# First loads, first norm and the mixer's projections as one program without barriers

## The reference, cut to what matters

```python
def rmsnorm(x, w):
    xf = x.astype(jnp.float32)
    y = xf * lax.rsqrt(jnp.mean(xf * xf, axis=-1, keepdims=True) + NORM_EPS)
    return (y * w.astype(jnp.float32)).astype(x.dtype)

def hybrid_mixer(h, w_in, ...):
    proj = (h @ w_in).astype(f32)
    ...

x = x + hybrid_mixer(rmsnorm(x, norm_mix_w[l]), w_in[l], ...)
x = x + memory_cross_attention(rmsnorm(x, norm_xa_w[l]), rmsnorm(mem, norm_mem_w[l]), ...)
x = x + peer_ffn(rmsnorm(x, norm_ffn_w[l]), ...)
```

## Time and profile before

| | us |
|---|---|
| median of 3 runs | 2443.94 |
| lowest and highest | 2443.73 to 2445.16 |
| profiled execution, its own time | 2442.29 |
| its span, first to last instruction | 2440.5 |
| PE busy | 2268.1 (93%) |
| DVE busy | 1551.4 (64%) |
| ACT busy | 1128.0 (46%) |

### The profile page before, as it was taken

One profiled execution on the slowest core, in us unless ns is written; L12 is line 12 of the kernel. 1 busy time (PEld: TensorE's weight loads), 2 busy tenths in 40 slices (PEclk: granted clock), 3 DMA queues, 4 the chain that ended last, 5 costly groups with the idle time before them and its releaser, 6 DMA issues. The chain is left out here.

```text
span 2440.5 us, 38520 instructions
## 1 busy us (share of the span) xinstructions
PE 2268.1 (93%) x15466; PEld 2085.1 (85%) x15466; DVE 1551.4 (64%) x2831; ACT 1128.0 (46%) x1966; POOL 74.5 (3%) x36
## 2 busy tenths in 40 slices
PE   5968888989999999999998999999999999878998
PEld 5967766989999998888887998979998899856998
DVE  5866354699888896666665546665546445494554
ACT  4532334444555445555554444444443444384443
POOL 0021000401000000000000000000000000000000
PEclk9988989989999999999998999999999999888999
DMA  5453232445444445656645555535555655303552
GB/s 219 148 67 79 104 138 73 158 143 174 155 147 148 147 148 164 196 192 194 194 156 217 189 189 208 193 135 209 188 192 183 232 184 185 118 18 121 190 187 106
DMA packets 78151, 389.74 MB, mean 160 GB/s; under 512 B 9739, under 2 KB 12683, under 8 KB 49580
## 3 DMA queue, kind: packets, MB, share of 16 engines
q1 hardware_dynamic: 76668, 383.13, 45.2%
q0 software_dynamic: 1040, 4.19, 1.6%
q10 hardware_dynamic: 288, 0.26, 0.0%
HBM read 382.31 MB, written 5.24 MB: 159 GB/s over the span
## 5 line engine op out<-in xcount | busy, mean ns | idle before, releaser
L246 DVE TENSOR_TENSOR split_slots<-ring,split_slots 128x1024 fp32r<-128x1024 f32 x396 | 468.2, 1228 | 333.1 <-ACT split_slots L237 333.1
L339 PE MATMUL banks<-x_transposed_hi,split_slots 128*128 128x256 f32 x1936 | 553.7, 286 | 14.9 <-PEq L417 5.7
L340 PE MATMUL banks<-x_transposed_lo,split_slots 128*128 128x256 f32 x1936 | 551.9, 285 | 0.0
L341 PE MATMUL banks<-x_transposed_hi,split_slots 128*128 128x256 f32 x1936 | 551.6, 285 | 0.0
L237 ACT ACTIVATE split_slots<-ring 128x1024 fp32r<-128x1024 f32 x406 | 404.3, 1049 | 222.1 <-PE banks L341 194.0
L350 DVE SCALAR_TENSOR_TENSOR expert_lo<-ring,expert_hi 128x512 fp32r<-128x512 f32 x512 | 360.3, 709 | 190.2 <-ACT expert_hi L345 189.1
L345 ACT ACTIVATE expert_hi<-ring 128x512 fp32r<-128x512 f32 x512 | 323.1, 632 | 276.5 <-PE banks L341 276.4
L339 PEld LDWEIGHTS banks<-x_transposed_hi,split_slots 128*128 128x128 f32 x1936 | 374.9, 194 | 17.8 <-issue 10.2
L340 PEld LDWEIGHTS banks<-x_transposed_lo,split_slots 128*128 128x128 f32 x1936 | 374.9, 194 | 1.5
L341 PEld LDWEIGHTS banks<-x_transposed_hi,split_slots 128*128 128x128 f32 x1936 | 374.8, 194 | 0.0
L339 PE MATMUL banks<-x_transposed_hi,expert_hi 128*128 128x256 f32 x1024 | 296.8, 290 | 17.7 <-DVE expert_lo L350 17.2
(11 more groups left out here) (468 smaller groups left out, 3469.2 us busy)
## 6 DMA issues: line engine op xcount, KB each, us to landing
ring<-in_ffn_w SPq DMA_DIRECT2D x132, 1024.0 KB, 4.8
ring<-in_peer_u SPq DMA_DIRECT2D x128, 512.0 KB, 3.5
ring<-in_peer_v SPq DMA_DIRECT2D x128, 512.0 KB, 4.2
ring<-in_w_in SPq DMA_DIRECT2D x16, 1024.0 KB, 5.0
ring<-in_sgu_w_in SPq DMA_DIRECT2D x16, 1024.0 KB, 4.8
ring<-in_peer_wq SPq DMA_DIRECT2D x8, 1024.0 KB, 5.1
ring<-in_sgu_w_out SPq DMA_DIRECT2D x8, 1024.0 KB, 4.7
ring<-in_kv_w SPq DMA_DIRECT2D x6, 1024.0 KB, 4.9
```

The lines of the kernel that those rows point to most:

```text
L246: ins = dve.tensor_tensor(self.parts[:, b, 1, p], self.k.w.slot(g)[:, p], self.parts[:, b, 0, p].bitcast(F32), ALU.subtract)
L339: pe.matmul(out, lh, rh, start=start, stop=False)
L340: pe.matmul(out, lh, rl, start=False, stop=False)
L341: return pe.matmul(out, ll, rh, start=False, stop=stop)
```

## The change

The three first stages share one block (`joined_stages`), so their two barriers are gone. x comes in two transfers, one for each tile, each with a semaphore of its own. The norm's weight is loaded as a row, spread over all partitions, into a part of `s.conv` that is not used yet, and is multiplied in while the row is scaled, on DVE before the transposes (`scalar_tensor_tensor`, two halves for each tile), where it was four instructions on the turned banks. The split of xT then reads PSUM directly. ident is asked for by ACT. The parameter columns and ones are asked for behind the ring slots and waited for where they are first used, and the mask constants and tables behind ring slots 3 to 5. Two of the four banks are split high before slot 0 and two behind it. Panel 0 runs by `high_first`. The lines behind the touched functions shift: in the changed kernel the transposes are line 513, and the matmuls of panel 0 are lines 320, 322 and those of `high_first`'s second loop.

```diff
--- before.py
+++ after.py
@@ -463,33 +463,41 @@
-def begin_program(k, s, bias, padded):
...
+class Begun:
+    def __init__(self, k):
+        self.x_landed = [k.sig.new() for _ in range(TILES)]
+        self.ident_landed, self.gain_landed, self.cols_landed, self.ones_landed, self.zeroed = (k.sig.new() for _ in range(5))
+        self.high, self.written = (k.sig.new() for _ in range(2))
+def begin_program(k, begun, gain, bias, padded):
+    a, block = k.a, k.open
+    consts = a["constants"].rearrange("p (c n) -> p c n", n=P)
+    @block.sync
+    def _(sp):
+        for i in range(TILES):
+            sp.dma_start(k.x[:, i, :], a["x"][0][i * P:(i + 1) * P, :]).then_inc(begun.x_landed[i], 16)
+        sp.dma_start(gain, a["norm_mix_w"].partition_broadcast(P).rearrange("p a d -> p (a d)")).then_inc(begun.gain_landed, 16)
+        k.w.issue(sp, RING)
+        sp.dma_start(k.cols[:, :], a["parameter_columns"]).then_inc(begun.cols_landed, 16)
+        sp.dma_start(k.ones[:, :], consts[:, C_ONES, :]).then_inc(begun.ones_landed, 16)
+    @block.scalar
+    def _(act):
+        act.dma_start(k.ident[:, :], consts[:, C_IDENT, :]).then_inc(begun.ident_landed, 16)
+    @block.vector
+    def _(dve):
+        dve.memset(k.eps[:, 0:1], EPS).then_inc(k.boot, 1)
+        dve.memset(k.eps[:, 1:2], LN_EPS).then_inc(k.boot, 1)
+        dve.memset(padded[:, :, 0:3], 0.0).then_inc(begun.zeroed, 1)
+        dve.memset(bias.table[32:33, :], NEG).then_inc(begun.zeroed, 1)
 COL_MIX, COL_XA, COL_MEM, COL_FFN, COL_CONV, COL_B1 = 0, 8, 16, 24, 32, 112
@@ -508,74 +516,52 @@
             ins.then_inc(ready, 1)
-def norm_transpose(k, jobs, loads=()):
...
+def first_norm(k, ctx, begun, xn, gain):
+    block = k.open
+    stat = k.sb(ctx, "row_stats", [P, 3, TILES])
+    warm = k.sb(ctx, "unused_root", [P, 1])
+    squared, rooted, recip, normed, banks = (k.sig.new() for _ in range(5))
+    highs, lows = split_turned(k, 4, k.xT, banks, begun.high, begun.written)
+    begin = Beginning(k)
+    @block.scalar
+    def _(act):
+        act.wait_ge(k.boot, 2)
+        act.activation(warm[:, :], k.eps[:, 0:1], ACT.Sqrt)
+        for i in range(TILES):
+            act.wait_ge(begun.x_landed[i], 16)
+            act.activation(xn[:, i, :], k.x[:, i, :], ACT.Square, accum_out=stat[:, 0, i:i + 1]).then_inc(squared, 1)
+            act.wait_ge(squared, i + 1)
+            act.activation(stat[:, 1, i:i + 1], stat[:, 0, i:i + 1], ACT.Sqrt, bias=k.eps[:, 0:1], scale=1.0 / D
+                           ).then_inc(rooted, 1)
+        highs(act, 0, 2)
+        begin.highs(act)
+        highs(act, 2, 4)
+    @block.vector
+    def _(dve):
+        for i in range(TILES):
+            dve.wait_ge(rooted, i + 1)
+            dve.reciprocal(stat[:, 2, i:i + 1], stat[:, 1, i:i + 1]).then_inc(recip, 1)
+            if i == 0:
+                dve.wait_ge(begun.gain_landed, 16)
+            dve.wait_ge(recip, i + 1)
+            for n in range(2):
+                own = slice(n * D // 2, (n + 1) * D // 2)
+                dve.scalar_tensor_tensor(xn[:, i, own], k.x[:, i, own], stat[:, 2, i:i + 1], gain[:, own],
+                                         ALU.mult, ALU.mult).then_inc(normed, 1)
+        lows(dve, 0, 2)
+        begin.lows(dve)
+        lows(dve, 2, 4)
+    @block.tensor
+    def _(pe):
+        pe.wait_ge(begun.ident_landed, 16)
+        for i in range(TILES):
+            turn_chunks(pe, k, xn[:, i, :], i, banks, 4, normed)
 def bank4(k, b):
@@ -589,13 +575,13 @@
 def split_turned(k, first, dst, banks, high, written):
-    def highs(act):
-        for b in range(4):
+    def highs(act, at=0, end=4):
+        for b in range(at, end):
             act.wait_ge(banks, b + 1)
             split_high(act, dst.hi[bank_part(b)], bank4(k, first + b)).then_inc(high, 1)
-    def lows(dve):
-        for b in range(4):
+    def lows(dve, at=0, end=4):
+        for b in range(at, end):
             dve.wait_ge(high, b + 1)
             split_low(dve, dst.lo[bank_part(b)], bank4(k, first + b), dst.hi[bank_part(b)]).then_inc(written, 1)
     return highs, lows
@@ -845,7 +831,7 @@
 MIXER_PANELS = 16
-def project_and_normalise(k, s, padded, memT):
+def project_and_normalise(k, s, begun, bias, padded, memT):
@@ -885,6 +871,10 @@
             for n, name in enumerate(("gdn_dt_bias", "gdn_a_log", "mlstm_i_bias", "mlstm_f_bias")):
                 sp.dma_start(row[:, n, :], k.a[name].partition_broadcast(P).rearrange("p a h -> p (a h)")
                              ).then_inc(gates_landed, 16)
+            k.w.issue(sp, 2 * RING)
+            sp.dma_start(s.consts[:, :, :], k.a["constants"].rearrange("p (c n) -> p c n", n=P)).then_inc(k.masks_landed, 16)
+            sp.dma_start(bias.table[0:32, :], k.a["rel_table_2"]).then_inc(k.table_landed, 16)
+            sp.dma_start(bias.onehot[:, :], k.a["bucket_onehot"]).then_inc(k.table_landed, 16)
             k.stream(sp)
         @block.tensor
@@ -894,6 +884,13 @@
                     pe.wait_ge(panel_read, m - 3)
                 split.ready(pe, m)
                 wh, wl = split.panel(m)
+                if m == 0:
+                    own = [slice(j * P, (j + 1) * P) for j in range(2)]
+                    high_first(pe, Before(None, (begun.high, 4), (begun.written, 4)),
+                               lambda j: k.psum[:, 0, j * SEQ:(j + 1) * SEQ],
+                               lambda j, c: ((wh[:, c, own[j]], wl[:, c, own[j]]), k.xT.at(slice(0, P), c)), True
+                               ).then_inc(split.eaten, 1)
+                    return
                 for j in range(2):
                     own = slice(j * P, (j + 1) * P)
                     for c in range(DC):
@@ -915,6 +912,7 @@
             def norms():
                 pe.wait_ge(squared, 2)
+                pe.wait_ge(begun.ones_landed, 16)
                 for b in KEYS_FIRST:
                     if b == 0:
                         pe.wait_ge(narrow_read, 1)
@@ -1028,7 +1026,6 @@
         @block.gpsimd
         def _(pool):
-            k.sig.clear_other(pool)
             pool.wait_ge(mem_low, 4)
             for n in range(2):
                 pool.wait_ge(shaped, 2 * n + 2)
@@ -1041,6 +1038,9 @@
         def _(dve):
             def convolve(item):
                 dve.wait_ge(panel_read, item + 1)
+                if item == 0:
+                    dve.wait_ge(begun.zeroed, 1)
+                    dve.wait_ge(begun.cols_landed, 16)
                 for tap in range(4):
                     for q in range(2):
                         n = 2 * item + q
@@ -3616,10 +3616,14 @@
             memT = Split(k, core, "memory_T", [P, DC, SEQ])
             with ExitStack() as inner:
                 padded = k.sb(inner, "conv_input_T", [P, 20, 3 + SEQ])
-                begin_program(k, s, bias, padded)
                 inner.enter_context(k.lasting_splits())
-                norm_transpose(k, [(k.x, k.xT, COL_MIX)])
-                project_and_normalise(k, s, padded, memT)
+                rows = s.conv[:, 0:12, :].rearrange("p a n -> p (a n)")
+                gain, xn = rows[:, 0:D], rows[:, D:3 * D].rearrange("p (i d) -> p i d", i=TILES)
+                with k.joined_stages():
+                    begun = Begun(k)
+                    begin_program(k, begun, gain, bias, padded)
+                    first_norm(k, inner, begun, xn, gain)
+                    project_and_normalise(k, s, begun, bias, padded, memT)
             s.more(k, core)
             key_query_products(k, s, bias)
             gdn_prepare(k, s, bias)
@@ -3647,7 +3651,7 @@
 _NAMES = ["x", "mem", "gdn_a_log", "gdn_dt_bias", "gdn_norm_w", "mlstm_i_bias", "mlstm_f_bias",
-          "mlstm_norm_w", "norm_xa_w", "norm_ffn_w", "peer_v", "norm_final_w", "rel_table_2", "ln_g_2", "ln_b_2", "sgu_ln_g_2",
+          "mlstm_norm_w", "norm_mix_w", "norm_xa_w", "norm_ffn_w", "peer_v", "norm_final_w", "rel_table_2", "ln_g_2", "ln_b_2", "sgu_ln_g_2",
           "sgu_ln_b_2", "sgu_b_s_2", "cmp_w2_2"]
```

More of the change, by code:

```diff
@@ L508, in turn_chunks @@
             ins.then_inc(ready, 1)
-def norm_transpose(k, jobs, loads=()):
[L514 to L569, removed]
-        @block.tensor
-        def _(pe):
-            for e in range(TILES * N):
-                n, i = divmod(e, TILES)
-                pe.wait_ge(normed, e + 1)
-                turn_chunks(pe, k, xn[n][:, i, :], i, banks, 4 * n)
-        k.idle_pool(block)
```

## The result

| us | before | changed |
|---|---|---|
| median | 2443.84 | 2427.97 |
| lowest to highest (4 runs each) | 2443.44 to 2445.16 | 2425.51 to 2430.28 |
| profiled execution, its own time | 2442.29 | 2430.28 |
| its span | 2440.5 | 2428.5 |
| first matmul of panel 0, in the profile | 28.13 | 14.64 |

The ratio is 0.9937, with a 95% interval of 0.9925 to 0.9949: faster, by 15.9 us in the median. The 2429.7 forecast lies inside its spread. Two later series of the same kernel gave medians of 2430.54 and 2429.68 (5 runs each) against 2444.36 and 2444.64 for the kernel before. Over all 14 runs the median of the changed kernel is 2429.6.

The account below looks back on a forecast made before the run. PE bounds the panels, but ahead of them 9 us are a wait for bytes and 13 us an ACT and DVE chain. Panel 0 starts at 13.9, not 28.13: 2443.94 - 14.2 = 2429.7, range 2426.5 to 2433.5.

Parts of the forecast that it names:

- The place: Stage ahead of panel 0: its first matmul comes 14.2 us earlier, and everything behind follows PE and shifts as a whole.
- The arrival: First loads: tile 0 seen landed at 4.25, tile 1 at 5.75, weight row at 7.0, slot 0 at 10.1.
- The sum for the row: Weight row's landing, behind x: 1.25 us after the transfer ahead of it, taken as 7.0.
- What I costed at nothing: Table load, tile 1's sums, late low parts, mem, later slots and constants: all covered by other work, 0 us.
- the sum: Chain from loads to panel 0: first matmul at 13.9 instead of 28.13, median 2429.7; chance 0.55 for 2428 to 2431.5.
- the order of passes: Panel 0 by high_first: low parts of banks 2 and 3 are free; in the old order it starts 1.4 us later.
- The clock: Panel 0 starts at 1.2 GHz for as long as before, no difference; bounds 1.9 us gained, 1.5 us lost.
- Rival B: Panel 0 starts at full clock after only 2.55 us idle: 1.9 us more gained, 2427.8; chance 0.22.
- the rule weighed in the prediction: Ahead of panel 0: transposes do not count as PE busy, so panel 0 starts low, 2429.7; against it, 2427.8.
- A: First landings share the engines, the row landing with slot 0 at 10.1: 11.2 us gained, 2432.7; chance 0.19.
- D: Whole program: more time at 1.2 GHz behind short idle times; 40 us more gives 2449.7; chance 0.02.
- The number: Whole kernel: profiled execution 2428.1, median 2429.7.

Follow-up runs that it names:

- The barrier run: Changed kernel with the barrier between the first norm and the panels put back, SP waiting there for ones and the columns: 2432.01 us.
- the third series: Second repeat of the changed kernel with no edit, on the same chip as later experiments: median 2429.68 us.

## Why the prediction was right

**The place.** Right: all of the gain is ahead of panel 0, the work behind it is PE's and moves along, and ones behind the weights was the largest part (7.7 of 13.4 us by a run of its own).

**The arrival** was the term that was mis-sized. Tile 0's square began at 4.83 (forecast 4.25), the row was there at 7.78 (7.0), slot 0 at 2.14 + 8.1 = 10.24 (10.1). The rate of the earlier trace rows held from 4 to 6 us, but the microsecond after it has a hole:

```profile
4.00:6.00 2.00, 0.00 (x0) 0.00 (x0) 0.00 (x0) 1.15 (x2) 0.00 (x0) 1.00 1.03 407
6.00:7.00 1.00, 0.00 (x0) 0.00 (x0) 0.16 (x1) 0.99 (x2) 0.00 (x0) 1.00 0.74 238
```

The same microsecond in the kernel before:

```profile
6.00:7.00 1.00, 0.00 (x0) 0.00 (x0) 0.00 (x0) 0.00 (x0) 0.00 (x0) 1.00 0.87 369
```

What makes the hole is not shown. The sum for the row also left out ident's 0.07 MB, which landed at 0.75 + 4.2 = 4.95, ahead of it. And the two later loads that it was taken from were asked for 0.38 us apart (299.29 and 299.67) and not 0.45, which makes the second 1.2 us behind the first and not 1.25. The 0.78 us of the row went through the chain nearly unchanged: transposes at 8.68 for 7.85, slot 0's low half until 14.59 for 13.9, first matmul 14.64 for 13.9. So 13.5 us and not 14.2. The durations taken from rows held: scaling 1.41 for 1.42, transposes 3.65 for 3.49, splits 1.99 and 2.36.

**What I costed at nothing** was nothing: table load, tile 1's sums, low parts of banks 2 and 3, mem, slots 1 to 5, constants. The barrier run adds that mem could come 11 us later still and slot 3 four.

**Two steps reasoned past each other.** I gave x by tiles a landing of its own in the sum, though the sum itself shows tile 0 waiting for the row. The run with x in one transfer gives it 0.2 us. And I counted the order of passes as 1.4 us and the barriers as part of the whole; the runs show panel 0 starting 1.3 us later with the old order alone and 1.4 with the second barrier alone, so either of the two takes the whole saving away.

**The clock.** The sum took panel 0 as starting low for 4.2 us, with 1.9 us gained or 1.5 lost as bounds. Its length in the profiles was 8.37, 8.45 and 7.32 us against 7.70 before: 0.7 us lost, 0.8 lost and 0.4 gained, within the bounds. Rival B as written (all of panel 0 at full clock) came true in no profile without extra matmuls on PE; of the three of the changed kernel one started fast and fell. That the transposes leave the clock low, the rule weighed in the prediction (the Trainium skill, "TensorE: Matmul & The Clock Gate", "Part 4: PE-mode transpose"), does not hold in every execution here: in the third series nothing but 16 transposes ran on PE ahead of a panel 0 whose first matmuls went at 0.12 us each, though in the first two, behind the same transposes, they went at 0.21.

**Rivals A and D.** A is out: row and slot 0 landed one behind the other, 7.78 and 10.24. D had the right mechanism for the scatter (low stretches elsewhere shift) and no bias: 191 to 197 us at the low level, from 198. But not all low stretches stand behind idle times, as it had them: the one at the gates falls on a busy PE.

**The number.** The profiled execution was forecast at 2428.1 and came at 2430.28, 0.7 us by the row, 0.7 by panel 0, and 0.8 by later stretches. The median of its four runs, 2427.97, is lower than that of all 14, 2429.6. That the forecast of 2429.7 meets the latter within 0.1 us is luck: 0.7 us of arrival were mis-sized, and the clock moves a single execution by several us.

## What to carry to other kernels

Look first at what the first wait counts: a small transfer behind megabytes on the same queue holds up everything that shares its semaphore, and moving it ahead took one line and brought 7.7 us here. A tile that lands early is worth little (0.2 us here) while the other operand of its first use stands behind it. And when the profile says that PE is busy, read the pace of its matmuls too: here a block of 48 narrow ones, 5.3 us at their full pace of 0.111 us, cost another 3.4 to 5.1 us by the low clock that began within it, and was better dealt out between wide ones.

## What the runs showed of the hardware

In each of the 12 profiles that have the gates as one block, 48 matmuls of 16 columns in a row on a PE that shows as busy throughout, the clock falls to 1.2 GHz within the block and stays there for 6.8 or 10.2 us (before: 25 matmuls in 3.00 us, then 27 in 5.60 us).

```profile
85.00:88.00 3.00, 3.00 (x25) 3.00 (x24) 3.00 (x6) 1.92 (x3) 0.00 (x0) 0.83 0.42 178
88.00:93.60 5.60, 5.60 (x27) 5.60 (x27) 5.60 (x12) 0.00 (x0) 0.00 (x0) 0.50 0.60 196
```

Dealt out between 48 matmuls of 256 columns, the same 48 bring no fall, in both profiles that have them so (clock 1.00 from 60 to 90 us and beyond). I had not looked at that block before, since PE's row was full. Nor had I expected a fall in the middle of dense matmuls, 1.7 us after panel 0 began.
